# Dilated attention on one Trainium2 core: long and short sequences in turn, the operand splits spread over more steps, and the keys' high halves made by GpSimd

## The chip, the core and the metric

The program runs on one core of a Trainium2 chip. A core has TensorE (PE: matrix products; PEld is its weight load), VectorE (DVE), ScalarE (ACT), GpSimd (POOL) and SyncE (SP, here an issuer of transfers). Each runs its own list of instructions in order; they meet only at semaphores. The metric is the device time in microseconds (us). Before the change three runs took 4597.08, 4600.01 and 4615.36 us: median 4600.01.

## The reference, cut to what matters

One encoder layer over two sequences, of 1024 and 2048 tokens: a projection, a state-space branch, an attention branch, an output projection. The change is in the attention. It computes three windowed attentions of dilation 1, 4 and 16, for 16 heads of 64 channels, and mixes them:

```python
DILATED_PATTERNS = ((128, 1), (512, 4), (2048, 16))
def dilated_window_attention(q, k, v, window, dilation):
    r = window // (2 * dilation)              # 64 keys to either side, in a subsequence
    ...                                       # to_sub: every dilation-th token
    scores = jnp.einsum('nbqhd,nbkhd->nbhqk', qb, kw) * (HEAD_DIM ** -0.5)
    valid = ((jnp.abs(qi[:, :, None] - ki[:, None, :]) <= r)
             & (ki[:, None, :] >= 0) & (ki[:, None, :] < l_sub))
    scores = jnp.where(valid[None, :, None], scores, -jnp.inf)
    lse = jax.nn.logsumexp(scores, axis=-1)
    p = jnp.exp(scores - lse[..., None])
    o = jnp.einsum('nbhqk,nbkhd->nbqhd', p, vw)
```

## The kernel before, in words

The program runs in phases with a barrier between them: projection, convolution, state-space phases, attention, output. Only attention changes.

Attention handles two heads at a time, so there are eight **pairs**. For a pair it works through six **stretches**: one sequence (s = 1 is the 2048-token one, called long here; s = 0 the 1024-token one, short) at one dilation. "Long 4" below is the long sequence at dilation 4. `attention_stretches` sets their order: long 1, long 4, long 16, short 1, short 4, short 16, then the next pair. A long stretch has 8 **steps**, a short one 4; a step handles two tiles of 128 queries for both heads. There are 288 steps. At dilation 1 and 4 a tile of queries meets 256 keys (**banded** steps), at dilation 16 a subsequence has at most 128 tokens, so it meets 128 (**narrow** steps, half the transposes and half the output products).

The score products run in single passes on numbers split in two, high + low. So before a stretch starts, four **pieces** have to be split: query half 0, query half 1, key half 0, key half 1. ScalarE casts the piece to the high part (`split_high`, L1509 to L1518), and GpSimd subtracts it from the original (`split_low`, L1367 to L1373), both reading `nat`, the untouched q and k of the pair, with a stride of the dilation (4 or 16 tokens). A long piece has 1024 elements in each of 128 partitions, a short one 512. Query and key operands have two buffers, used by stretches in turn. `pieces_at` (L1328) says at which step of a stretch the pieces of the next one are made: one in each of the steps 0 to 3 of a long stretch, two in each of the steps 0 and 1 of a short one.

The engines' lists of a step n are:

- TensorE: `turn(n)` transposes the probabilities (L1477), `scores(n + 2)` (L1465), `outputs(n - 1)` (L1493). Before the first scores of a stretch it waits for all four pieces (`a_low`), so that wait stands in step F - 2, where F is the first step of that stretch.
- VectorE: copies the transposed probabilities out of PSUM (L1572), then mask and row minimum of step n + 2 (L1562).
- ScalarE: `copy_o(n - 2)` (L1534), the casts of this step (L1517), then four exponentials of step n + 2 (L1527).
- GpSimd: the subtractions; and at the end of every second stretch one of 16 pieces of the output weights: it issues the load (L1604), waits for it, and splits it with two instructions (L1607, L1610).
- SyncE: loads of `nat` (L1393) and v (L1408, L1413), stores of the outputs (L1425, L1430).

## Time and profile before

| | us |
|---|---|
| median of three runs | 4600.01 |
| the profiled execution | 4615.0 |
| its span, first to last instruction | 4613.4 |
| TensorE busy | 4027.3 |
| VectorE busy | 2015.6 |
| GpSimd busy | 1712.5 |
| ScalarE busy | 1502.0 |

The page of the profile gives busy time of each engine, and the span in 40 slices of 115 us, each digit a share in tenths. Attention is slices 25 to 34 (from zero). The line PEclk is the clock granted to TensorE, in tenths of its full 2.4 GHz: 5 is 1.2 GHz. Matrix products are pipelined and their ends are modelled, so TensorE counts as busy at either clock; how fast it gets on is seen from the count of instructions in a stretch of time. A row of the timeline has start, length, engine, line, operation, the tiles, and in brackets how long the engine was idle before it and who ended that.

### The profile page before, as it was taken

What the parts mean: (1) busy time and instruction counts of PE and PEld (TensorE: products, weight loads), DVE (VectorE), ACT (ScalarE), POOL (GpSimd) and SP (SyncE); (2) the same over time, 40 slices, a digit from 0 to 9 for tenths busy, and PEclk for the clock granted to TensorE, in tenths of its full rate; (3) what the DMA queues carried; (4) which work ended last, traced back from release to release, by engine and by line L of the source; (5) the groups of instructions that cost most, each with busy time, mean ns of one, the idle gap of its engine ahead of it and who ended that gap; (6) DMA issues with size and microseconds to landing.
All of it is one profiled execution on the core that took longest, in us unless ns stands there. A gap on an engine that the chain in (4) does not pass through costs nothing. (4 is left out here: it accounts for less than half of the span.)

```text
span 4613.4 us, 57057 instructions
## 1 busy us (share of the span) xinstructions
PE 4027.3 (87%) x21637; PEld 3219.5 (70%) x21637; DVE 2015.6 (44%) x3716; ACT 1502.0 (33%) x2697; POOL 1712.5 (37%) x965
## 2 busy tenths in 40 slices
PE   6999999999999997325777775999999999799999
PEld 5888878888878886212333332889888898678887
DVE  2000220001300012976888885665565655555554
ACT  3212022121211110320222222776666766422222
POOL 2222432224312232005999997444443333200000
PEclk8999999999999998558888887997897887899999
DMA  5233232323322232557222222343333333434442
GB/s 174 95 98 99 90 125 90 99 94 90 112 91 96 98 108 90 174 168 266 76 92 87 86 93 99 86 116 98 97 112 103 95 101 82 138 142 158 161 157 106
DMA packets 358458, 523.73 MB, mean 114 GB/s; under 512 B 21947, under 2 KB 222723, under 8 KB 354115
## 3 DMA queue, kind: packets, MB, share of 16 engines
q1 hardware_dynamic: 348899, 484.07, 32.7%
q10 hardware_dynamic: 4608, 19.92, 1.4%
q0 software_dynamic: 4736, 16.78, 1.0%
q8 instruction: 145, 2.38, 0.2%
q14 instruction: 70, 0.57, 0.0%
HBM read 336.42 MB, written 184.27 MB: 113 GB/s over the span
## 5 line engine op out<-in xcount | busy, mean ns | idle before, releaser
L313 POOL TENSOR_TENSOR project_w_lo<-project_raw,project_w_hi 128x1024 fp32r<-128x1024 f32 (+1 forms) x204 | 381.1, 1878 | 1001.6 <-ACT project_w_hi L371 1001.6
L443 DVE TENSOR_TENSOR project_part<-project_out,project_table 128x512 f32<-128x512 f32 x48 | 33.2, 691 | 1524.8 <-PE project_out L500 1128.5
L1493 PE MATMUL attn_o_ps<-attn_v,attn_pt_sb 128*128 128x65 f32 x3840 | 557.2, 302 | 0.0
L1527 ACT ACTIVATE attn_p_sb<-attn_p_sb,attn_o_sb 128x256 f32<-128x256 f32 (+1 forms) x1152 | 451.1, 465 | 311.8 <-DVE attn_o_sb L1562 311.8
L1493 PEld LDWEIGHTS attn_o_ps<-attn_v,attn_pt_sb 128*128 128x128 f32 x3840 | 515.3, 214 | 36.2 <-issue 5.7
L1572 DVE COPY attn_pt_sb<-attn_pt_ps 128x1024 f32<-128x1024 f32 (+1 forms) x288 | 301.4, 1047 | 354.6 <-PE attn_pt_ps L1477 354.2
L1562 DVE CUSTOM_DVE_ANT_0 attn_p_sb<-attn_mask,attn_s_ps 128x256 f32<-128x256 bf16 (+1 forms) x1152 | 363.8, 371 | 130.6 <-PE attn_s_ps L1465 112.9
L1371 POOL TENSOR_TENSOR attn_q_lo<-attn_nat,attn_q_hi 128x1024 fp32r<-128x1024 f32 (+1 forms) x96 | 199.0, 2084 | 529.2 <-ACT attn_q_hi L1517 529.2
L500 PE MATMUL project_out<-project_h_hi,project_w_hi 128*128 128x512 f32 x1344 | 339.0, 395 | 29.3 <-DVE project_h_lo L431 29.3
L1024 PE MATMUL ssd_seg<-ssd_spread,masks 128*128 128x512 f32 x384 | 253.7, 803 | 94.5 <-POOL ssd_spread L963 94.4
L500 PE MATMUL project_out<-project_h_hi,project_w_lo 128*128 128x512 f32 x1344 | 334.7, 391 | 0.0
L500 PE MATMUL project_out<-project_h_lo,project_w_hi 128*128 128x512 f32 x1344 | 332.1, 389 | 0.0
L963 POOL TENSOR_TENSOR ssd_spread<-masks,st_a 128x512 f32<-128x512 f32 x192 | 311.3, 1650 | 5.4 <-DMA ssd_skip<-d_skip 4.0
L500 PEld LDWEIGHTS project_out<-project_h_hi,project_w_hi 128*128 128x128 f32 x1344 | 254.1, 190 | 83.1 <-issue 21.1
L371 ACT CAST project_w_hi<-project_raw 128x1024 fp32r<-128x1024 f32 (+1 forms) x204 | 167.7, 845 | 398.4 <-DMA project_raw<-w_in 398.4
L1477 PE MATMUL attn_pt_ps<-ident,attn_p_sb 128*128 128x128 f32 x1920 | 292.4, 297 | 2.1 <-ACT attn_p_sb L1527 2.0
L500 PEld LDWEIGHTS project_out<-project_h_hi,project_w_lo 128*128 128x128 f32 x1344 | 254.6, 189 | 53.8
L500 PEld LDWEIGHTS project_out<-project_h_lo,project_w_hi 128*128 128x128 f32 x1344 | 252.3, 188 | 52.4
L500 PE MATMUL project_out<-project_w_hi,project_h_lo 128*128 128x512 f32 x1152 | 284.5, 389 | 0.0
L500 PE MATMUL project_out<-project_w_hi,project_h_hi 128*128 128x512 f32 x1152 | 284.5, 389 | 0.0
L500 PE MATMUL project_out<-project_w_lo,project_h_hi 128*128 128x512 f32 x1152 | 284.5, 389 | 0.0
L1465 PE MATMUL attn_s_ps<-attn_k_hi,attn_q_hi 64*128 64x256 f32 (+1 forms) x1152 | 204.5, 351 | 74.8 <-POOL attn_k_lo L1371 74.8
(186 smaller groups left out, 6794.0 us busy)
## 6 DMA issues: line engine op xcount, KB each, us to landing
project_raw<-w_in SPq DMA_DIRECT2D x156, 512.0 KB, 4.0
output_parts<-s_o SPq DMA_DIRECT2D x24, 1584.0 KB, 6.5
s_o<-attn_o_sb SPq DMA_DIRECT2D x256, 132.0 KB, 2.0
s_xbcT<-project_stage SPq DMA_DIRECT2D x72, 256.0 KB, 2.0
back_xb<-s_xb ACTq DMA_DIRECT2D x24, 640.0 KB, 6.1
ssd_xb<-s_xb SPq DMA_DIRECT2D x24, 640.0 KB, 4.0
s_v<-project_v_stage SPq DMA_DIRECT2D x48, 260.0 KB, 2.2
s_zs<-project_stage SPq DMA_DIRECT2D x48, 256.0 KB, 2.2
```

What stands on the lines that cost most here:

```text
L313: last = nc.gpsimd.tensor_tensor(low, src, high.bitcast(F32), ALU.subtract)
L371: last = nc.scalar.copy(dst, src)
L500: last = nc.tensor.matmul(dst, lhs, rhs, start=x == 0 and k == 0, stop=x == 2 and k == KT - 1)
L963: last = nc.gpsimd.tensor_tensor(spread[d][b][:, :, :], mask.to_broadcast([P, 4, P]), per_head(chunk_row("a", n)[:, at:at + 4], P), ALU.mult)
L1024: last = nc.tensor.matmul(seg[b][:, :], st["masks"][:, d, :], spread[d][b][:, :, :], start=d == 0, stop=d == 1)
L1371: nc.gpsimd.tensor_tensor(split_cuts(low[st.buf], st, piece, keys), nat_cut(st, piece), split_cuts(high[st.buf], st, piece, keys).bitcast( ...
L1465: last = nc.tensor.matmul(s_ps[n % 2][:, 2 * half + a, 0:st.width], qs[st.buf][rows, queries], ks[st.buf][rows, keys], start=x == 0, stop= ...
L1477: last = nc.tensor.transpose(pt_ps[:, x, cut], p_sb[n % 2][:, x, cut], c["ident"][:, :])
L1493: last = nc.tensor.matmul(o_ps[n % 2][:, x, :], pt_sb[n % 2][:, x, b * P:(b + 1) * P], v[st.buf][:, st.chunk(r, t, b), half * VW:(half + 1 ...
L1527: last = nc.scalar.activation(cut, cut, ACT.Exp, scale=-1.0, bias=o_sb[n % ring][:, x % 2, x // 2, VW:OW])
L1562: nc.vector.tensor_tensor_reduce(out=p_sb[n % 2][:, x, 0:st.width], in0=mask[:, st.strip(t), 0:st.width], in1=s_ps[n % 2][:, x, 0:st.width ...
L1572: nc.vector.tensor_copy(pt_sb[n % 2][:, :, 0:st.width], pt_ps[:, :, 0:st.width]).then_inc(sem["a_pt"], 1)
```

## The change

- The order of stretches is now long 1, short 1, long 4, short 4, long 16, short 16. The split of the next stretch is always made beside one of the other length.
- `splits_at` replaces `pieces_at`. While stretch S (first step F) runs, the next one's pieces are made at steps F - 2, F, F + 2, F + 4 if S is long, and at F - 2, F - 1, F, F + 1 if S is short. The list begins two steps ahead of S itself.
- ScalarE casts only the query pieces. GpSimd makes the high part of a key piece with a `tensor_copy` of its own right ahead of the subtraction; it first waits for both query casts.
- The loads of the output weights are issued by SyncE in step 1 of every long stretch, and GpSimd splits them in step 5; the loop that finished what was left is gone. The loads of `nat` are issued at step 0 of a dilation-16 stretch, for the same sequence of the next pair.

```diff
@@ attention_stretches
-        for s in (1, 0):
-            for pattern in range(len(DILATIONS)):
+        for pattern in range(len(DILATIONS)):
+            for s in (1, 0):
                 stretches.append(Stretch(len(stretches), pair, s, pattern, first))
@@ attention_phase
-        def pieces_at(st, i):
-
-            if st.number + 1 == len(stretches):
-                return ()
-            if st.steps == 4:
-                return ((0, 1), (2, 3), (), ())[i]
-            return (i,) if i < pieces else ()
...
+        splits_at = [[] for _ in steps]
+        for st, following in zip(stretches, stretches[1:]):
+            for piece in range(pieces):
+                splits_at[max(0, st.first - 2 + piece * (2 if st.steps > pieces else 1))].append((following, piece))
@@ gpsimd
             def split_low(st, piece):
                 high, low = ((q_hi, q_lo), (k_hi, k_lo))[piece // 2]
-                pool.wait_ge(sem["a_high"], pieces * st.number + piece + 1)
                 keys = piece // 2 == 1
+                pool.wait_ge(sem["a_key_high" if keys else "a_high"], 2 * st.number + piece % 2 + 1)
...
+            def split_keys_high(st, piece):
+                if piece < 2:
+                    return
+                pool.wait_ge(sem["a_high"], 2 * (st.number + 1))
+                if st.number >= 2 and piece == 2:
+
+                    older = stretches[st.number - 2]
+                    pool.wait_ge(sem["a_scores"], older.first + older.steps)
+                nc.gpsimd.tensor_copy(split_cuts(k_hi[st.buf], st, piece, True), nat_cut(st, piece)
+                                      ).then_inc(sem["a_key_high"], 1)
...
             for n, (st, i) in enumerate(steps):
-                for piece in pieces_at(st, i):
-                    split_low(stretches[st.number + 1], piece)
-                if i == st.steps - 1 and st.number % 2 == 1:
-                    out_weights.load_and_split_next(pool)
-            out_weights.finish_first_half(pool)
+                for following, piece in splits_at[n]:
+                    split_keys_high(following, piece)
+                    split_low(following, piece)
+                if st.steps > pieces and i == st.steps - 3:
+                    out_weights.split_next(pool)
+            pool.wait_ge(sem["first_w_split"], out_weights.pieces)
@@ sync
-                    sp.wait_ge(sem["a_low"], pieces * (st.number - per_round + 3))
+                    sp.wait_ge(sem["a_low"], pieces * (st.number - per_round + 5))
...
-                if i == 1 and st.pattern == 2 and st.number + per_round - 2 < len(stretches):
-                    load_nat(stretches[st.number + per_round - 2])
+                if i == 0 and st.pattern == 2 and st.number + 2 < len(stretches):
+                    load_nat(stretches[st.number + 2])
+                if st.steps > pieces and i == 1:
+                    out_weights.load_next(sp)
@@ scalar
             def split_high(st, piece):
-                dst = (q_hi, k_hi)[piece // 2][st.buf]
+                if piece >= 2:
+                    return
...
-                nc.scalar.copy(split_cuts(dst, st, piece, piece // 2 == 1), nat_cut(st, piece)
+                nc.scalar.copy(split_cuts(q_hi[st.buf], st, piece, False), nat_cut(st, piece)
                                ).then_inc(sem["a_high"], 1)
```

GpSimd's list, before: from the split of pair 1's long 1 (the last of pair 0) to that of its long 4. Rows with 128x1024 belong to a long stretch.

```order
L1371 TENSOR_TENSOR attn_q_lo<-attn_nat,attn_q_hi 128x1024 [waits a_high] x2
L1371 TENSOR_TENSOR attn_k_lo<-attn_nat,attn_k_hi 128x1024 [waits a_high] x2
L1604 DMA out_weights_raw<-w_out 128x512 [waits first_w_split]
L1607 TENSOR_TENSOR out_weights_hi<-out_weights_raw,one 128x512 [waits first_w_in]
L1610 TENSOR_TENSOR out_weights_lo<-out_weights_raw,out_weights_hi 128x512 [waits first_w_hi]
L1371 TENSOR_TENSOR attn_q_lo<-attn_nat,attn_q_hi 128x1024 [waits a_high] x2
L1371 TENSOR_TENSOR attn_k_lo<-attn_nat,attn_k_hi 128x2x512 [waits a_high] x2
```

And after: the split of a long 4 (made beside short 1), that of short 4 (beside long 4), and one piece of the output weights.

```order
L1364 TENSOR_TENSOR attn_q_lo<-attn_nat,attn_q_hi 128x1024 [waits a_high] x2
L1376 CAST attn_k_hi<-attn_nat 128x2x512 [waits a_scores,a_high]
L1364 TENSOR_TENSOR attn_k_lo<-attn_nat,attn_k_hi 128x2x512 [waits a_key_high]
L1376 CAST attn_k_hi<-attn_nat 128x2x512 [waits a_high]
L1364 TENSOR_TENSOR attn_k_lo<-attn_nat,attn_k_hi 128x2x512 [waits a_key_high]
L1364 TENSOR_TENSOR attn_q_lo<-attn_nat,attn_q_hi 128x512 [waits a_high] x2
L1376 CAST attn_k_hi<-attn_nat 128x2x256 [waits a_scores,a_high]
L1364 TENSOR_TENSOR attn_k_lo<-attn_nat,attn_k_hi 128x2x256 [waits a_key_high]
L1376 CAST attn_k_hi<-attn_nat 128x2x256 [waits a_high]
L1364 TENSOR_TENSOR attn_k_lo<-attn_nat,attn_k_hi 128x2x256 [waits a_key_high]
L1624 TENSOR_TENSOR out_weights_hi<-out_weights_raw,one 128x512 [waits first_w_in]
L1627 TENSOR_TENSOR out_weights_lo<-out_weights_raw,out_weights_hi 128x512 [waits first_w_hi]
```

A stretch's split had four GpSimd instructions and has six now: two casts stand between its subtractions. Long and short splits alternate.

ScalarE's list, before, in short 16 of pair 0, where long 1 of pair 1 is made: a COPY opens a step, four ACTIVATE close it.

```order
L1534 COPY attn_o_sb<-attn_o_ps 128x2x2x65 [waits a_o]
L1517 CAST attn_q_hi<-attn_nat 128x1024 [waits a_scores,a_keys_set,a_nat_in1]
L1517 CAST attn_q_hi<-attn_nat 128x1024
L1527 ACTIVATE attn_p_sb<-attn_p_sb,attn_o_sb 128x128 [waits a_max] x4
L1534 COPY attn_o_sb<-attn_o_ps 128x2x2x65 [waits a_o]
L1517 CAST attn_k_hi<-attn_nat 128x1024 x2
L1527 ACTIVATE attn_p_sb<-attn_p_sb,attn_o_sb 128x128 [waits a_max] x4
```

The same split after; these are now the last two steps of long 16.

```order
L1542 COPY attn_o_sb<-attn_o_ps 128x2x2x65 [waits a_o]
L1525 CAST attn_q_hi<-attn_nat 128x1024 [waits a_scores,a_nat_in1]
L1535 ACTIVATE attn_p_sb<-attn_p_sb,attn_o_sb 128x128 [waits a_max] x4
L1542 COPY attn_o_sb<-attn_o_ps 128x2x2x65 [waits a_o]
L1525 CAST attn_q_hi<-attn_nat 128x1024
L1535 ACTIVATE attn_p_sb<-attn_p_sb,attn_o_sb 128x128 [waits a_max] x4
```

The query casts moved two steps ahead and lie one step apart; the key casts are gone from this engine.

## Rows read from the trace of the kernel before

**Rows 1.** The page: busy time by engine, and TensorE's granted clock in 40 slices.
```profile
PE 4027.3 (87%) x21637; PEld 3219.5 (70%) x21637; DVE 2015.6 (44%) x3716; ACT 1502.0 (33%) x2697; POOL 1712.5 (37%) x965
...
PEclk8999999999999998558888887997897887899999
```
**Rows 2.** Windows: busy us (instructions) by engine, granted clock, DMA share, GB/s.
```profile
core 0: us, PE busy (x) PEld busy (x) DVE busy (x) ACT busy (x) POOL busy (x), PEclk, DMA share, GB/s
...
2880.40:3993.80 1113.40, 1072.70 (x9216) 978.16 (x9216) 652.67 (x2592) 755.12 (x1628) 433.62 (x236) 0.86 0.35 97
```
**Rows 3.** Windows: eight banded steps, four narrow ones; three banded, one narrow.
```profile
2917.71:2947.45 29.74, 29.74 (x294) 27.35 (x293) 18.71 (x73) 21.76 (x48) 14.96 (x8) 1.00 0.36 95
...
3108.32:3129.00 20.68, 20.68 (x110) 19.01 (x110) 8.04 (x27) 10.13 (x19) 7.17 (x5) 0.50 0.19 46
2949.03:2958.20 9.17, 9.17 (x98) 8.21 (x98) 5.99 (x35) 6.90 (x22) 2.68 (x3) 1.00 0.77 261
3148.50:3152.73 4.23, 4.23 (x25) 3.78 (x26) 1.61 (x9) 3.50 (x7) 2.96 (x3) 0.50 0.51 108
```
**Rows 4.** TensorE's waits in attention: us in total, times, longest.
```profile
PE attn_s_ps L1465 <- POOL attn_k_lo L1371: 38.2, 18, 4.9
```
**Rows 5.** Timeline: TensorE's wait in pair 1's short 1, twice at short 16.
```profile
3103.27 0.58 PE L1465 MATMUL attn_s_ps<-attn_k_hi,attn_q_hi 64*128 64x256 f32 x2 [2.27 <-POOL attn_k_lo L1371]
...
3008.43 0.58 PE L1465 MATMUL attn_s_ps<-attn_k_hi,attn_q_hi 64*128 64x256 f32 x2 [4.88 <-POOL attn_k_lo L1371]
...
3154.87 0.58 PE L1465 MATMUL attn_s_ps<-attn_k_hi,attn_q_hi 64*128 64x256 f32 x2 [1.08 <-POOL attn_k_lo L1371]
```
**Rows 6.** Windows: stretches of granted half clock in attention, and one of full clock.
```profile
2973.20:2980.10 6.90, 6.90 (x40) 6.34 (x40) 2.07 (x9) 2.08 (x5) 2.36 (x3) 0.51 0.32 82
...
3014.20:3102.90 88.70, 86.64 (x851) 78.84 (x848) 61.77 (x243) 70.45 (x151) 36.88 (x19) 1.00 0.38 108
3102.90:3161.00 58.10, 56.65 (x305) 51.79 (x306) 19.86 (x82) 24.72 (x54) 21.30 (x15) 0.50 0.32 84
...
3249.70:3270.20 20.50, 20.50 (x110) 18.83 (x110) 6.81 (x26) 9.45 (x19) 5.87 (x6) 0.50 0.20 56
...
3287.30:3307.70 20.40, 16.59 (x94) 14.71 (x94) 7.60 (x28) 9.89 (x18) 10.30 (x7) 0.50 0.32 81
...
3393.10:3396.50 3.40, 3.40 (x20) 3.07 (x21) 0.81 (x3) 1.40 (x4) 2.30 (x2) 0.50 0.18 59
```
**Rows 7.** Timeline of pair 0's long 4, first step: TensorE turns, then scores.
```profile
2913.99 1.04 PE L1477 MATMUL attn_pt_ps<-ident,attn_p_sb 128*128 128x128 f32 x8
2914.97 0.39 PE L1465 MATMUL attn_s_ps<-attn_k_hi,attn_q_hi 64*128 64x256 f32 x2
```
**Rows 8.** The same stretch, ScalarE: the casts of two neighbouring steps.
```profile
2914.82 1.97 ACT L1517 CAST attn_q_hi<-attn_nat 128x1024 fp32r<-128x1024 f32 x1
...
2918.56 1.97 ACT L1517 CAST attn_q_hi<-attn_nat 128x1024 fp32r<-128x1024 f32 x1
```
**Rows 9.** The same stretch, GpSimd: the second subtraction.
```profile
2920.61 2.89 POOL L1371 TENSOR_TENSOR attn_q_lo<-attn_nat,attn_q_hi 128x1024 fp32r<-128x1024 f32 x1 [0.86 <-ACT attn_q_hi L1517]
```
**Rows 10.** Timeline before the 4.88 us wait, dilation 1: casts, then subtractions.
```profile
2997.95 1.99 ACT L1517 CAST attn_q_hi<-attn_nat 128x1024 fp32r<-128x1024 f32 x2
```
**Rows 11.** The same place, GpSimd's subtractions of the keys.
```profile
3003.72 4.66 POOL L1371 TENSOR_TENSOR attn_k_lo<-attn_nat,attn_k_hi 128x1024 fp32r<-128x1024 f32 x2
```
**Rows 12.** GpSimd by shape, in attention: busy us, mean ns of one, idle before.
```profile
L1371 POOL TENSOR_TENSOR attn_k_lo<-attn_nat,attn_k_hi 128x1024 fp32r<-128x1024 f32 x48 | 130.2, 2719 | 35.4 <-ACT attn_k_hi L1517 35.4
...
L1607 POOL TENSOR_TENSOR out_weights_hi<-out_weights_raw,one 128x512 fp32r<-128x512 f32 x16 | 16.5, 1031 | 47.9 <-DMA out_weights_raw<-w_out 47.9
...
L1350 POOL MEMSET attn_k_hi<- 128x2560 f32 x2 | 4.5, 2232 | 12.5 <-POOLq L866 12.5
```
**Rows 13.** The loads of nat: time from issue to landing.
```profile
DMA to landing us min/median/max: 4.2/6.2/11.3
```

More of the change, by code:

```diff
@@ L1326, in nat_cut @@
             return rows[:, half * st.dil // 2:(half + 1) * st.dil // 2, :]
-        def pieces_at(st, i):
-            if st.number + 1 == len(stretches):
-                return ()
-            if st.steps == 4:
-                return ((0, 1), (2, 3), (), ())[i]
-            return (i,) if i < pieces else ()
-        def nat_ready(st, pattern=0):
-            return st.number // per_round + 1
+        splits_at = [[] for _ in steps]
+        for st, following in zip(stretches, stretches[1:]):
+            for piece in range(pieces):
+                splits_at[max(0, st.first - 2 + piece * (2 if st.steps > pieces else 1))].append((following, piece))
         def v_ready(st):
@@ L1373, in split_low @@
                                         ).then_inc(sem["a_low"], 1)
+            def split_keys_high(st, piece):
[7 more added lines that the diff above has]
+                                      ).then_inc(sem["a_key_high"], 1)
             for piece in range(pieces):
+                split_keys_high(stretches[0], piece)
                 split_low(stretches[0], piece)
             for n, (st, i) in enumerate(steps):
-                for piece in pieces_at(st, i):
-                    split_low(stretches[st.number + 1], piece)
-                if i == st.steps - 1 and st.number % 2 == 1:
-                    out_weights.load_and_split_next(pool)
-            out_weights.finish_first_half(pool)
+                for following, piece in splits_at[n]:
[4 more added lines that the diff above has]
+            pool.wait_ge(sem["first_w_split"], out_weights.pieces)
         @block.sync
@@ L1434, in _ @@
             load_v(stretches[0])
-            load_nat(stretches[3])
+            load_nat(stretches[1])
             for n, (st, i) in enumerate(steps):
@@ L1508, in split_high @@
             def split_high(st, piece):
-                dst = (q_hi, k_hi)[piece // 2][st.buf]
+                if piece >= 2:
+                    return
                 if piece == 0:
                     act.wait_ge(sem["a_nat_in"][st.s], 32 * (st.number // per_round + 1))
-                    act.wait_ge(sem["a_keys_set"], 2)
                     if st.number >= 2:
@@ L1542, in _ @@
                 copy_o(n - 2)
-                for piece in pieces_at(st, i):
-                    split_high(stretches[st.number + 1], piece)
+                for following, piece in splits_at[n]:
+                    split_high(following, piece)
                 exponentials(n + 2)
@@ L1594, in __init__, with cut, load_next, split_next @@
         self.pieces = D_SSD // P * D // CW
-        self.next = 0
-    def load_and_split_next(self, pool):
-        nc, sem, n = self.nc, self.sem, self.next
+        self.loaded = self.split = 0
+    def cut(self, n):
+        return n // 2, slice(n % 2 * CW, (n % 2 + 1) * CW)
+    def load_next(self, sp):
+        if self.loaded == self.pieces:
+            return
+        k, cols = self.cut(self.loaded)
+        after(sp, self.sem["first_w_split"], self.loaded)
+        sp.dma_start(self.raw[:, :], self.rows[:, k, cols]).then_inc(self.sem["first_w_in"], 16)
+        self.loaded += 1
+    def split_next(self, pool):
+        nc, sem, n = self.nc, self.sem, self.split
         if n == self.pieces:
             return
-        k, cut = n // 2, slice(n % 2 * CW, (n % 2 + 1) * CW)
-        after(pool, sem["first_w_split"], n)
-        pool.dma_start(self.raw[:, :], self.rows[:, k, cut]).then_inc(sem["first_w_in"], 16)
+        k, cols = self.cut(n)
         pool.wait_ge(sem["first_w_in"], 16 * (n + 1))
-        nc.gpsimd.tensor_tensor(self.hi[0][:, k, cut], self.raw[:, :], self.one.to_broadcast([P, CW]), ALU.mult
+        nc.gpsimd.tensor_tensor(self.hi[0][:, k, cols], self.raw[:, :], self.one.to_broadcast([P, CW]), ALU.mult
                                 ).then_inc(sem["first_w_hi"], 1)
         pool.wait_ge(sem["first_w_hi"], n + 1)
-        nc.gpsimd.tensor_tensor(self.lo[0][:, k, cut], self.raw[:, :], self.hi[0][:, k, cut].bitcast(F32), ALU.subtract
+        nc.gpsimd.tensor_tensor(self.lo[0][:, k, cols], self.raw[:, :], self.hi[0][:, k, cols].bitcast(F32), ALU.subtract
                                 ).then_inc(sem["first_w_split"], 1)
-        self.next += 1
-    def finish_first_half(self, pool):
-        while self.next < self.pieces:
-            self.load_and_split_next(pool)
-        pool.wait_ge(self.sem["first_w_split"], self.pieces)
+        self.split += 1
 def output_phase(nc, sem, c, x_parts, y_parts, weights, norm_f, scratch):
@@ L1898 @@
     "f_scaled", "f_rest", "f_cb", "f_zeroed", "f_added", "f_norm_steps", "f_root", "f_m_part", "f_kept",
-    "f_y_steps", "a_keys_set", "a_mask_steps", "a_high", "a_low", "a_scores", "a_max", "a_p", "a_turned", "a_pt",
+    "f_y_steps", "a_keys_set", "a_mask_steps", "a_high", "a_key_high", "a_low", "a_scores", "a_max", "a_p", "a_turned", "a_pt",
     "a_o", "a_o_copied", "first_w_split", "first_w_hi", "first_w_in",
```

## The prediction

> **What bounds the kernel now.** I read the page first: TensorE is busy for 87% of the span, and its granted clock falls in places from slice 25 on, where attention runs [rows 1]. A window over attention, first to last score product, gives 1113.4 us, with a mean clock of 0.86 [rows 2]. So I asked two things: what a step costs at each clock, and what TensorE waits for.
>
> At full clock eight banded steps take 29.74 us, 3.72 each, and four narrow ones 9.17, 2.29 each; TensorE has no gap in either window. At half clock three banded steps take 20.68, 6.89 each, and a narrow one 4.23 [rows 3]. No other engine sets a step. A pair has 24 banded and 12 narrow steps, 24 x 3.72 + 12 x 2.29 = 116.8 us, and eight pairs 934. Attention takes 1113, so 179 us are lost, and they have two names.
>
> The first: TensorE waits 38.2 us in 18 waits, all for GpSimd's last key subtraction [rows 4]. Eight of them are the 2.27 us kind, in step 2 of short 1, where short 4's scores begin. Three are 4.88 us and some 1.08, in short 16, where the next pair's long 1 begins [rows 5]; three are 0.27.
>
> The second: half clock. Each of the eleven waits of 2.24 us or more ends in it, and the clock falls nowhere else in attention. The 2.27 us wait ends at 3103.27, and half clock is granted from 3102.90 to 3161.00; the full-clock stretch ahead of it, 88.7 us long, holds no wait of note [rows 5, 6]. The 1.08 us waits stand inside such stretches. They last 58 us four times (pairs 1, 4, 5, 6), 20.5 twice, 3.4 once and 6.9 four times, 303 us in all. At half clock the engine does 3.72/6.89 = 0.54 of the work, so 0.46 x 303 = 139 us are lost. With 38.2 that is 177, which closes the account. The small waits are cheap; what follows them is not.
>
> The clock comes back in banded steps, sometimes after one and sometimes not after five; in narrow steps at half clock it never did: the 58 us stretches run through the narrow steps of short 16 and end when the banded scores of the next long 1 are back.
>
> **Order of stretches.** Score, transpose and output work is the same, 934 us. The old order gave a long stretch's split the 8 steps of another long one, except once a pair. Now each of the three long splits has to be made beside a short stretch, in 4 steps.
>
> **A long split beside a short banded stretch** (long 4 beside short 1, long 16 beside short 4). The two query casts fall in neighbouring banded steps, as before in long 4's preparation of long 16. There the first of the two steps begins at 2913.99 and TensorE is ready for scores 0.98 later [rows 7]. The casts start at 2914.82 and 2918.56 [rows 8], and the second query subtraction ends at 2920.61 + 2.89 = 2923.50 [rows 9]. Then come, on GpSimd alone and one behind the other, cast c, subtraction 2.9, cast c, subtraction 2.9, and some 0.2 for the two waits between them: done at 2929.5 + 2c. TensorE asks four steps after the first begins: 2913.99 + 4 x 3.72 + 0.98 = 2929.85. The wait is 2c - 0.3, with about 0.1 of semaphore 2c - 0.2.
>
> What is c, a strided fp32 cast of 1024 elements on GpSimd? The trace before has no such operation. From below, the memset: 2232 ns for 2560 elements [rows 12], so 0.95 us for 1024, with no input read. From above the strided two-input subtraction itself, 2.9 [rows 9]; the multiply by a broadcast value, 1031 ns for 512 [rows 12], makes 2.0. The cast reads one stream where the multiply also reads a constant, but it reads with a stride. I take 1.6, between memset and multiply, and 1.1 where the dilation is 1. The wait is then 3.0 us, between 1.7 and 5.6.
>
> The Trainium skill, GPSIMD Engine Reference, section 3.1, puts loops that read one input at 1.03 cycles per element, some 1.0 us for 1024 elements. By that estimate c is 1.0, the wait 1.8, and the sum 19 us less. The same section's 2.6 cycles for two inputs gives 2.3 us, and the dilation-1 subtraction took that: 4.66 for two [rows 11].
>
> **The long split beside short 16.** Before, casts start at 2997.95 [rows 10], and TensorE asks at 3008.43 - 4.88 = 3003.55, 5.6 later. The list now starts two narrow steps sooner, so 5.6 + 4.6 = 10.2 us are there. Needed are the second query subtraction (its cast waits for the next step) by 6.4, then two of 2.33 [rows 11] and two casts of 1.1: 13.5. It would be a wait of 3.3 us at full clock; at half clock four steps last 17 us and there is none.
>
> **Short splits** beside a long stretch have 8 steps for some 10 us of work: hidden, 18.4 us of waits gone at short 1, and short 16's too.
>
> **What a wait drags behind it.** The wait for long 16 stands in step 2 of short 4. By all eleven cases before, a wait of 3.0 us drops the clock. What follows is one and a half banded steps, then the twelve narrow steps of long 16 and short 16 together, where half clock has never ended [rows 3, 6]. The price: 1.5 x 3.17 + 12 x 1.94 = 28 us, with the wait 31 per pair.
>
> The wait for long 4 stands in step 2 of short 1; ten banded steps follow. Seven of the eleven stretches before were short, 10 us in the mean: 3.0 + 0.46 x 10 = 7.6 us. The other four lasted 58: 3.0 + 27 = 30. Two thirds and one third give 15; I take 13, since a long one swallows the wait for long 16. Together 44 a pair, 352 us for eight.
>
> **Small parts.** ScalarE loses 96 key casts, 125 us of its work, but no step waits for it: nothing. At the start, GpSimd's first split grows by two casts ahead of the first scores: + 2 us. The output weights' loads leave GpSimd (16 issues of 0.6 us) and no longer make it wait for them; they stand on SyncE's queue ahead of a store, whose output ring of six gives cover: nothing; without that cover 24 x 0.5 us. The load of `nat` for the next short 1 is issued at the start of short 16 and wanted two steps on, with a landing of 4.2 to 11.3 us [rows 13] against some 6.5 at full clock and 12 at half. At half clock, where I expect narrow steps, it is hidden; else up to 3 us for seven pairs, 21.
>
> **The sum.** Against the profiled execution: 4615 - 177 + 352 + 2 = 4792. That execution lies 15 us over the median of 4600, because the length of the half-clock stretches varies; the sum replaces them all, so I leave the 15 in the uncertainty. Forecast 4790 us, slower by 4%, own range 4745 (all stretches behind long 4's wait short: 8 x 38.6 = 309) to 4840 (half of them long: 398).
>
> **Rivals.** First, the other side: faster. The new waits do not drop the clock, because they come out near 1.7 us, and nothing before lies between 1.08, which stood in half clock already, and 2.24. Then 16 x 3.0 + 8 x 3.3 = 74 us are lost, and fewer if c is small: 4615 - 177 + 74 + 2 = 4514. It decides at the size of wait that still keeps the clock. For it: the waits would be smaller than any that fell. Against: c would have to be at memset's price. The Trainium skill, TensorE: Matmul & The Clock Gate, Part 1, section What's actually happening, says the ramp penalty is under 1% of a typical kernel's span; that would be 46 us here, and by it the result would be near 4560. This trace shows 139 us, 3%, so it does not hold here, and I give this side 12%.
>
> Second, half of them drop it (c near 1.0, waits of 1.8): between the two, (309 + 60) / 2 = 185, so about 4645: 12%.
>
> Third, the strided cast is as dear as the subtraction: waits of 5.6, 16 x 2.6 = 42 more, 4832: 13%.
>
> Fourth, half clock is caught in the banded steps as well, from short 1 to the next long 1, as it was for five steps in four pairs: 12 x 3.17 + 28 + 3 = 69 us a pair, 552: about 4990. Against: in ten steps it has longer to come back. 8%.
>
> **How the numbers follow.** My forecast has 55%. Faster is the first rival, 12%; a measurement of this kernel tells 0.5%, 23 us, and within that lies only part of the second, 3%; slower holds 85%. The range 4640 to 4880 leaves out the first and the fourth, 20%.
>
> **What would show it.** In the profile after: TensorE waits for the key subtraction in step 2 of short 1 and of short 4 in each pair, 2 to 4 us, and no longer for short splits; GpSimd's cast of 128x1024 at 1.0 to 2.0 us; half clock granted over long 16 and short 16 with about 50 us for their twelve steps in most pairs; attention near 1290 us; ScalarE's busy time down by 125 us. I am wrong if the cast is under 0.9 us, if those waits are there and the clock stays, or if narrow steps at half clock win it back.

## The result, and the profile after

Four runs of the changed kernel took 4790.22 to 4820.89 us, median 4807.27; four of the kernel before on the same chip 4595.44 to 4615.36, median 4598.55. The ratio is 1.0448, with a 95% interval of 1.0406 to 1.0490: slower. The forecast was 4790, range 4640 to 4880. A run over 1.5% above the fastest of its kernel counts as slow (four of after_lead3's ten below, two of order_spread's ten, one each of weights_only's and wait_banded's); the ratios, and the spreads told below, leave such runs out, the medians are of all runs.

The profiled execution took 4819.63 us. The page of the kernel after:

```profile
PE 4221.9 (88%) x21637; PEld 3396.1 (70%) x21637; DVE 2014.1 (42%) x3716; ACT 1396.6 (29%) x2601; POOL 1827.2 (38%) x1045
...
PEclk8999999999999995578888866777877786589999
```

Beside [rows 1]: the same 21637 products keep TensorE busy for 195 us more, since more of them ran at a lower clock; ScalarE has 96 instructions fewer and GpSimd 80 more. Attention is slices 24 to 34 here (from zero), and the clock row is at 5 to 8 in every one of them, where the row before has a 9 in three. Windows of the kernel after, columns as in [rows 2]: the whole of attention (it runs to the last output product, as the window of [rows 2] does, 5 to 9 us beyond the last score product), then pieces of pair 1 (the wait before long 4's scores ends at 3111.93, the one before long 16's at 3163.76), then one of pair 0.

```profile
2875.97:4197.44 1321.47, 1266.17 (x9216) 1153.66 (x9216) 657.16 (x2592) 651.79 (x1534) 542.74 (x314) 0.72 0.30 82
3110.00:3120.20 10.20, 8.27 (x48) 7.69 (x48) 2.68 (x9) 2.08 (x5) 3.36 (x2) 0.50 0.22 57
3120.20:3164.60 44.40, 41.03 (x401) 37.57 (x397) 28.53 (x99) 27.16 (x59) 25.24 (x14) 1.00 0.31 83
3164.60:3236.30 71.70, 71.70 (x399) 64.54 (x398) 27.49 (x136) 29.76 (x80) 29.17 (x22) 0.50 0.37 104
3181.40:3215.20 33.80, 33.80 (x193) 30.21 (x193) 12.98 (x72) 15.24 (x42) 13.61 (x10) 0.50 0.29 80
2922.30:3072.50 150.20, 150.14 (x810) 136.97 (x812) 56.87 (x234) 58.36 (x139) 50.16 (x32) 0.50 0.26 72
```

Attention took 1321.5 us where it took 1113.4 [rows 2]: 208 us more, and the whole difference. It began 4.4 us sooner in this execution, and the output phase took 1.0 us more: 4615.4 - 4.4 + 208.1 + 1.0 = 4820.1, against 4819.6 measured. Its mean clock is 0.72 where it was 0.86. In pair 1 half clock lasts 10.2 us after the first wait, 44.4 us of full clock follow, and after the second wait it lasts 71.7 us; eight narrow steps in there take 33.80, 4.23 each, as in [rows 3]. TensorE's waits in attention, and the two of pair 1 (start, us, instruction, [idle before it and what ended it]):

```profile
PE attn_s_ps L1473 <- POOL attn_k_lo L1364: 53.8, 15, 3.8
```

```profile
3111.93 0.58 PE L1473 MATMUL attn_s_ps<-attn_k_hi,attn_q_hi 64*128 64x256 f32 x2 [3.77 <-POOL attn_k_lo L1364]
...
3163.76 0.33 PE L1473 MATMUL attn_s_ps<-attn_k_hi,attn_q_hi 64*128 64x128 f32 x2 [3.37 <-POOL attn_k_lo L1364]
```

Where 18 waits made 38.2 us [rows 4], 15 now make 53.8, and none of them stands before a short stretch: eight before long 4 (3.77 to 3.81 us), seven before long 16 (3.31 to 3.37). Each of the 15 is followed by half clock. GpSimd's timeline ahead of the first of the two shows what TensorE waited for; hardly a gap is left from 3101.90 on:

```profile
3099.06 2.89 POOL L1364 TENSOR_TENSOR attn_q_lo<-attn_nat,attn_q_hi 128x1024 fp32r<-128x1024 f32 x1 [0.90 <-ACT attn_q_hi L1525]
3101.90 2.07 POOL L1376 CAST attn_k_hi<-attn_nat 128x1024 fp32r<-128x1024 f32 x1
3104.05 2.88 POOL L1364 TENSOR_TENSOR attn_k_lo<-attn_nat,attn_k_hi 128x1024 fp32r<-128x1024 f32 x1
3106.87 2.08 POOL L1376 CAST attn_k_hi<-attn_nat 128x1024 fp32r<-128x1024 f32 x1
3109.03 2.85 POOL L1364 TENSOR_TENSOR attn_k_lo<-attn_nat,attn_k_hi 128x1024 fp32r<-128x1024 f32 x1
```

The account. Stretches of half clock in attention were 303 us before and are 729 now: 150.2 once (pair 0), 10.2 five times, 23.9 and 44.4 after long 4's waits; 61 to 96 (the last reaches 32 us beyond attention) after long 16's seven. 0.46 x 426 = 196, and 15.6 us more of waits: 212, against 208 measured.

### The profile page after: what moved, and what is told of

Its sections match the earlier page's. It is cut to its first block and busy times, and to the rows that moved or that the text cites. A ratio compares the mean times of both kernels' runs of the same rounds, so it can differ in the third digit from the quotient of the medians.

```text
span 4818.0 us, 57101 instructions
## 1 busy us (share of the span) xinstructions
PE 4221.9 (88%) x21637; PEld 3396.1 (70%) x21637; DVE 2014.1 (42%) x3716; ACT 1396.6 (29%) x2601; POOL 1827.2 (38%) x1045
## 5 line engine op out<-in xcount | busy, mean ns | idle before, releaser
L1501 PE MATMUL attn_o_ps<-attn_v,attn_pt_sb 128*128 128x65 f32 x3840 | 650.3, 335 | 0.0
L1501 PEld LDWEIGHTS attn_o_ps<-attn_v,attn_pt_sb 128*128 128x128 f32 x3840 | 604.2, 246 | 40.7 <-issue 6.3
L1485 PE MATMUL attn_pt_ps<-ident,attn_p_sb 128*128 128x128 f32 x1920 | 338.0, 327 | 1.1 <-ACT attn_p_sb L1535 1.1
L1473 PE MATMUL attn_s_ps<-attn_k_hi,attn_q_hi 64*128 64x256 f32 (+1 forms) x1152 | 231.6, 397 | 92.6 <-POOL attn_k_lo L1364 92.6
L1485 PEld LDWEIGHTS attn_pt_ps<-ident,attn_p_sb 128*128 128x128 f32 x1920 | 292.0, 184 | 1.6 <-ACT attn_p_sb L1535 1.4
```

What stands on the lines that cost most here:

```text
L1473: last = nc.tensor.matmul(s_ps[n % 2][:, 2 * half + a, 0:st.width], qs[st.buf][rows, queries], ks[st.buf][rows, keys], start=x == 0, stop= ...
L1485: last = nc.tensor.transpose(pt_ps[:, x, cut], p_sb[n % 2][:, x, cut], c["ident"][:, :])
L1501: last = nc.tensor.matmul(o_ps[n % 2][:, x, :], pt_sb[n % 2][:, x, b * P:(b + 1) * P], v[st.buf][:, st.chunk(r, t, b), half * VW:(half + 1 ...
```

## The experiments

All kernels are the changed one with edits; each was compared with the kernel before on its own chip (medians there: 4604.8, 4592.7 and 4604.8 us). "Waits" are TensorE's for the key subtraction within attention, "half" is granted half clock there; both come from the one profiled execution of each kernel, the medians from all runs.

| kernel | order | lead | keys | median us (runs) | ratio, 95% interval | attention | waits | half |
|---|---|---|---|---|---|---|---|---|
| before | old | 0 | ScalarE | 4599 (4) | 1 | 1113 | 38.2 | 311 |
| after | new | 2 | GpSimd | 4807 (4) | 1.0448 (1.0406 to 1.0490) | 1321 | 53.8 | 738 |
| spread_only | old | 2 | ScalarE | 4477 (4) | 0.9709 (0.9671 to 0.9748) | 975 | 11.5 | 47 |
| order_only | new | 0 | ScalarE | 4892 (4) | 1.0637 (1.0587 to 1.0686) | 1388 | 99.7 | 815 |
| keys_only | old | 0 | GpSimd | 4655 (4) | 1.0107 (1.0053 to 1.0161) | 1156 | 54.1 | 375 |
| order_spread | new | 2 | ScalarE | 4604 (10) | 0.9962 (0.9917 to 1.0007) | 1108 | 30.7 | 309 |
| spread_keys | old | 2 | GpSimd | 4467 (4) | 0.9694 (0.9641 to 0.9748) | 968 | 9.1 | 42 |
| weights_only | old | 0 | ScalarE | 4603 (10) | 0.9973 (0.9930 to 1.0015) | 1119 | 40.5 | 316 |
| lead3 | old | 3 | ScalarE | 4451 (6) | 0.9680 (0.9640 to 0.9720) | 953 | 0 | 13 |
| order_lead3 | new | 3 | ScalarE | 4471 (4) | 0.9725 (0.9673 to 0.9777) | 974 | 12.0 | 58 |
| order_lead3_w3 | new | 3 | ScalarE | 4440 (4) | 0.9636 (0.9585 to 0.9687) | 940 | 1.3 | 4 |
| after_lead3 | new | 3 | GpSimd | 4597 (10) | 0.9946 (0.9900 to 0.9992) | 1039 | 29.1 | 162 |
| wait_narrow | old | 3 | ScalarE | 4645 (4) | 1.0104 (1.0049 to 1.0159) | 1152 | 25.8 | 416 |
| wait_banded | old | 3 | ScalarE | 4534 (5) | 0.9863 (0.9797 to 0.9930) | 1062 | 26.9 | 201 |

"Lead" is the step rule: 0 is the old one (pieces begin with the stretch before), 2 the changed one, 3 starts one step sooner still beside short stretches. The model of the prediction, 934 us + waits + 0.46 x half, gives each of the fourteen to within 21 us, eleven of them to within 8 (order_only, 1409 against 1388, is the worst). The half clock of the table counts in 3 to 9 us at attention's very start, which the 303 and 729 above leave out.

Of the twelve expectations below seven gave a range that holds the measured median. order_spread landed between the two ranges given for it, order_lead3 6 us above its range, wait_banded 6 us below, order_lead3_w3 10 us under the one value given; after_lead3 came out 87 us above its range.

### One part of the change at a time

The three switches, as edits of the changed kernel (the new order's own load rules for `nat` go with the first):

```diff
-        for pattern in range(len(DILATIONS)):
-            for s in (1, 0):
+        for s in (1, 0):
+            for pattern in range(len(DILATIONS)):
...
-splits_at[max(0, st.first - 2 + piece * (2 if st.steps > pieces else 1))]
+splits_at[st.first + (piece if st.steps > pieces else piece // 2)]
...
-                    split_keys_high(following, piece)
                     split_low(following, piece)
...
-                if piece >= 2:
-                    return
+                dst = (q_hi, k_hi)[piece // 2][st.buf]
```

**spread_only**: first and third (old order, ScalarE's key casts; the new step rule stays).

> The old order of stretches and the key casts on ScalarE, with the new step rule (a split starts two steps before the running stretch) and the new loading of the output weights. Clock theory (each wait of 2 us or more for GpSimd drops TensorE to half clock, and that is what costs): short 1 now makes short 4 in four banded steps with a lead of 14.9 + 1.0 us against some 13 of work, and short 16 makes long 1 with 10.2 us against 9.4 + 1.1 of work plus the pause between the query casts; the waits fall from 2.27 and 4.88 us to about 0 and 1, no fall of the clock follows, and of the 177 us lost in attention 130 to 160 come back: 4440 to 4480 us. Rival (half clock is the narrow steps' own doing, the waits only mark the place): the 2.27 us waits go but the clock still falls at the end of long 16; only some 30 us come back, 4570.

**order_only**: second and third.

> The new order of stretches alone, with the old step rule (two pieces in each of the first two steps of a short stretch) and the key casts on ScalarE. Clock theory: a long split beside a short one has only two steps of lead, 7.4 + 1.0 us, and takes 2.1 + 4 x 2.9 = 13.7, so TensorE waits 5.5 to 6.5 us for long 4 and for long 16 in every pair, and half clock holds through the narrow steps: slower than the whole change, 4830 to 4900 us. Rival (the key casts on GpSimd are what costs, the order is harmless): within 30 us of before, 4600.

**keys_only**: first and second.

> The old order and the old step rule, with the keys' high parts cast by GpSimd. Clock theory: GpSimd's chain for short 4 grows by two casts of 1.1 us, so the wait in short 1 grows from 2.27 to 4 us, that in short 16 from 4.88 to 6 to 7; the number of falls of the clock stays, a third one may come for short 16: 20 to 70 us slower than before, 4620 to 4670. Rival (GpSimd's casts are the cost of the whole change): most of the 209 us, 4750 or more.

**order_spread**: third alone.

> The whole change with the key casts left on ScalarE. The casts then lie in four neighbouring steps beside GpSimd's subtractions, and the last subtraction of a long split ends about 1.2 us after TensorE asks, instead of 3.4 to 3.8. It asks whether a wait between 1.1 and 2 us drops the clock. If it does: half clock through the narrow steps again, 4720 to 4790. If it does not: waits of 16 x 1.2 and small ones, 4470 to 4500.

TensorE's waits in attention of spread_only, order_only, keys_only and order_spread, in that order:

```profile
PE attn_s_ps L1460 <- POOL attn_k_lo L1364: 11.5, 14, 1.1
```
```profile
PE attn_s_ps L1460 <- POOL attn_k_lo L1364: 99.7, 22, 6.3
```
```profile
PE attn_s_ps L1473 <- POOL attn_k_lo L1364: 54.1, 22, 4.0
```
```profile
PE attn_s_ps L1460 <- POOL attn_k_lo L1364: 30.7, 21, 1.9
```

The step rule alone makes the kernel 128 us faster, within the range that the clock theory gave. GpSimd's key casts alone, in the old order with the old step rule, cost 50 us (4605 to 4655, a ratio of 1.0107), with 22 waits of 1.5 to 4.0 us. The order alone makes it 288 us slower: the long splits beside short stretches, started as late as the old step rule starts them, wait about 6 us (6.05 before long 4, 5.8 before long 16). Order and step rule together undo each other, to no difference. And with them in place GpSimd's casts cost the last 203 us by the medians of two chips (4604 to 4807; the ratios, 0.9962 and 1.0448, part by 4.9%), with 15 waits of 3.3 to 3.8 us where 21 of 1.1 to 1.9 stood.

**spread_keys**: the first switch alone (old order; step rule and GpSimd's casts stay).

> The old order, the new step rule with its lead of two, key casts on GpSimd: the whole change without the new order. Beside short 1, short 4's pieces are 512 long: 0.8 + 1.1 + 2 x 1.5 within two steps, then 2 x (1.1 + 1.5): done before TensorE asks, so the 0.2 to 0.7 us of the kernel with casts on ScalarE go. Before long 1 the chain is two casts of 1.04 longer, but the query casts only, without keys, come sooner: a wait of 1.1 to 3. Clock theory: 4460 to 4510 us, since only banded steps follow. Rival (GpSimd's 125 us of casts cost by themselves): 4600.

```profile
PE attn_s_ps L1473 <- POOL attn_k_lo L1364: 9.1, 12, 1.1
```

4467 against spread_only's 4477 on another chip, with ratios of 0.9694 and 0.9709: in the old order the same 96 casts on GpSimd cost nothing, though its busy time in attention rises from 427 to 545 us. So it is not GpSimd's load that hurts but where its list is short of time: a strided long split beside a short stretch. Where the casts have eight steps they are free. So they are before long 1, which short 16 still makes: TensorE's wait stays at 1.1 us, since the two casts without a stride, 1.04 us each, fill the 1.27 and 0.83 us in which GpSimd waited for ScalarE's key casts in spread_only.

**weights_only**: all three switches undone; only the output weights' loading by SyncE is left, with their split by GpSimd moved to step 5 of a long stretch.

> The kernel before with only the output weights' loads issued by SyncE and their split in step 5 of a long stretch, all the rest as before. The waits in short 1 and short 16 are not touched: the same time as before within the spread of the half-clock stretches, 4580 to 4620 us. If the transfers or GpSimd's issuing had cost anything: faster by 10 us or more beyond that.

No difference, as priced. But two of its waits speak on the clock. One in pair 4, and the window around it:

```profile
3533.95 0.39 PE L1460 MATMUL attn_s_ps<-attn_k_hi,attn_q_hi 64*128 64x256 f32 x2 [2.24 <-POOL attn_k_lo L1364]
```
```profile
3450.00:3560.00 110.00, 107.11 (x1056) 97.75 (x1052) 72.93 (x289) 84.68 (x186) 49.44 (x28) 1.00 0.40 111
```

The size of wait that dropped the clock every time before [rows 5, 6] kept it here, and again 130 us later.

### Take the waits away, then put one back

**lead3**: old order, ScalarE's key casts, and the splits beside a short stretch one step sooner.

```diff
-st.first - 2 + piece * (2 if st.steps > pieces else 1)
+st.first - (2 if st.steps > pieces else 3) + piece * (2 if st.steps > pieces else 1)
```

> The old order, key casts on ScalarE, the new step rule with one change: beside a short stretch the four pieces start three steps ahead of it, not two. The waits of the kernel with a lead of two (0.2 to 0.7 us in short 1, 1.1 us in short 16, of which three of seven dropped the clock) should be gone: a banded step more is 3.7 us, a narrow one 2.3. Clock theory: no wait, no fall, attention at its 934 us and some 12 for its start: 4445 to 4455 us. Rival (with GpSimd out of the way another engine or a transfer becomes the bound): as with a lead of two, 4470 to 4480.

No wait for the key subtraction is left. What is left is TensorE's waits for ScalarE's exponentials, which neither the prediction nor the model counts, and one of them, 0.81 us, is followed by 10.2 us of half clock:

```profile
PE attn_pt_ps L1472 <- ACT attn_p_sb L1522: 7.6, 14, 1.1
```
```profile
3194.22 0.65 PE L1472 MATMUL attn_pt_ps<-ident,attn_p_sb 128*128 128x128 f32 x4 [0.81 <-ACT attn_p_sb L1522]
```

They are most of what attention of lead3 takes beyond the model (953 against 940):

```profile
2881.09:3833.66 952.57, 943.81 (x9216) 860.36 (x9216) 648.95 (x2592) 749.83 (x1628) 427.20 (x220) 0.99 0.41 113
```

**wait_narrow**: lead3, and GpSimd makes the last key subtraction of long 16 twice more in each pair. The repeats write the same numbers.

```diff
+repeats = 2 if piece == 3 and st.s == 1 and st.pattern == 2 and st.number > 0 else 0
-nc.gpsimd.tensor_tensor(...).then_inc(sem["a_low"], 1)
+for n in range(repeats + 1):
+    last = nc.gpsimd.tensor_tensor(...)      # each repeat waits for the one before
+last.then_inc(sem["a_low"], 1)
```

> The kernel with the old order and the lead of three, and in each pair GpSimd repeats the last key subtraction of long 16 twice, 5.8 us more ahead of long 16's scores, of which some 2.6 are covered: one wait of about 3.2 us a pair, right ahead of the eight narrow steps. Nothing else differs. Clock theory: the clock falls and stays down over all eight narrow steps, 1.5 x 3.17 + 8 x 1.94 + 3.2 = 23.5 us a pair, and longer where the banded steps of the short sequence do not bring it back: 190 us and up, 4640 to 4680. Rival (a wait costs its own length): 8 x 3.2 = 26 us, 4475.

**wait_banded**: the same with `st.pattern == 1`: the wait stands before long 4, with banded steps behind it.

> The same repeat for long 4 instead of long 16: the same wait of about 3.2 us, once in pairs 1 to 7 and in pair 0, but with ten banded steps behind it. Clock theory: the clock falls each time, and comes back after 7 to 58 us, at a point that the place of the wait in time decides: 3.2 + 0.46 x 10 = 8 us to 30 us a pair, 60 to 200 in all, and on the low side since narrow steps follow only later: 4540 to 4600, clearly under the kernel with the wait ahead of the narrow steps. Rival (where the wait stands does not matter): the same time as that kernel.

Waits of wait_narrow, and its second stretch of half clock:

```profile
PE attn_s_ps L1467 <- POOL attn_k_lo L1368: 25.8, 8, 3.2
```
```profile
3079.20:3130.40 51.20, 50.50 (x284) 45.80 (x284) 18.18 (x90) 22.68 (x57) 15.89 (x13) 0.50 0.27 85
```

The same of wait_banded, with a short and a long stretch:

```profile
PE attn_s_ps L1467 <- POOL attn_k_lo L1368: 26.9, 8, 3.4
```
```profile
3158.20:3168.40 10.20, 9.10 (x51) 8.32 (x52) 3.10 (x12) 2.08 (x5) 6.13 (x4) 0.50 0.05 13
3284.50:3390.30 105.80, 105.24 (x566) 96.10 (x568) 39.13 (x162) 45.39 (x101) 28.62 (x19) 0.50 0.21 64
```

This is the core of the explanation, shown by itself. Eight waits of 3.2 us ahead of narrow steps cost 4645 - 4451 = 194 us, 24 each: 3.2 for the wait itself and 21 for what follows it, some 51 us of half clock (0.46 x 51 would be 23), which in all eight pairs lasts through the eight narrow steps and ends in the banded steps of short 1. Eight waits of the same size ahead of banded steps cost 83 by the median, and are a gamble: in the profiled execution six are followed by 7 to 10 us of half clock, one by 41, one by 106, and the runs spread over 43 us (4520 to 4564) where wait_narrow's spread over 7. So it is not the added work on GpSimd, the same in both, that sets the price, but what runs behind the wait.

**order_lead3**: new order, lead 3, ScalarE's key casts.

> The new order of stretches with the lead of three steps and the key casts on ScalarE. It asks whether the order costs anything where no wait is left. With a lead of two the waits were 1.1 us before long 4 and long 16; 3.7 us more cover them. Clock theory: as the old order with the same lead, 4450 to 4465 us. Rival (the alternation itself costs: loads of nat late for short 1, v loads for a long stretch beside a short one): 4500 or more, with TensorE waiting for something that is not GpSimd.

It leaves seven waits, 2.34 us in five of the seven short 16. GpSimd's timeline shows why:

```profile
2988.11 2.37 POOL L1364 TENSOR_TENSOR attn_q_lo<-attn_nat,attn_q_hi 128x1024 fp32r<-128x1024 f32 x1 [1.25 <-ACT attn_q_hi L1512]
2990.45 1.03 POOL L1611 TENSOR_TENSOR out_weights_hi<-out_weights_raw,one 128x512 fp32r<-128x512 f32 x1
2991.56 1.28 POOL L1614 TENSOR_TENSOR out_weights_lo<-out_weights_raw,out_weights_hi 128x512 fp32r<-128x512 f32 x1
2992.80 2.37 POOL L1364 TENSOR_TENSOR attn_q_lo<-attn_nat,attn_q_hi 128x1024 fp32r<-128x1024 f32 x1
```

The output weights' split, 2.3 us in step 5 of long 16, stands between two query pieces of the next long 1. (There are 16 such pieces, one in each long stretch, so the last falls in pair 5's long 1; the two short 16 after that wait 0.17 and 0.18 us.) **order_lead3_w3** moves it two steps sooner:

```diff
-if st.steps > pieces and i == st.steps - 3:
+if st.steps > pieces and i == st.steps - 5:
```

> The new order with the lead of three and key casts on ScalarE, and the output weights' split in step 3 of a long stretch instead of step 5, where it stood for 2.3 us between GpSimd's first and second query piece of the next long 1 and made TensorE wait 2.34 us in five of seven pairs. If that was the whole cost of the order: no wait, no fall, 4450 us, as the old order with the same lead. If not: 4470 again.

```profile
2877.20:3816.90 939.70, 936.02 (x9216) 854.45 (x9216) 650.86 (x2592) 749.66 (x1628) 427.12 (x220) 1.00 0.42 115
```
```profile
PE attn_s_ps L1460 <- POOL attn_k_lo L1364: 1.3, 7, 0.3
```

4439.65 us (4438.00 to 4443.46), ratio 0.9636: the fastest kernel of the study, faster than the kernel before and than the changed one, with attention at 939.7 us where the steps alone make 934. The new order shows no cost once next to no wait is left in it. Whether it is better than the old one is not shown: the old order with the weights' split moved too was not run, and lead3's waits for ScalarE (7.6 us) are 1.3 us here.

**after_lead3**: the whole change, GpSimd's casts included, with lead 3 and the weights' split moved.

> The whole change, all three parts kept, with the pieces beside a short stretch started three steps ahead instead of two; the output weights' split moves from step 5 to step 3 of a long stretch, out of the way of the first piece. The waits before long 4 and long 16 were 3.77 and 3.37 us; a banded step more is 3.72, so 0 to 0.1 is left. Before long 1, 10.2 + 2.3 us of lead stand against 13.5 of work: 1.0 us, of which a few drop the clock for some 10 us in banded steps. Clock theory: 4455 + 7 x 1 + 3 x 5 = 4475, 4460 to 4510 us, over 300 us under the change. Rival (GpSimd's key casts or the order cost by themselves): 4600 or more. Rival (nat for short 1 comes late once narrow steps run at full clock): TensorE waits for ScalarE or the queries at short 16, 4500 to 4540.

```profile
PE attn_s_ps L1473 <- POOL attn_k_lo L1364: 29.1, 21, 2.2
```

Here I was wrong: I expected 0 to 0.1 us of wait, by one more banded step of 3.72. Measured were 21 waits: eight before long 4 (1.32 to 1.62 us), eight before long 16 (0.84 to 0.89), five before long 1 (2.22). The first query cast may not start before the scores of the stretch that last used its buffer are done. That is the long stretch two back, and TensorE makes its last scores in that very step; so the lead of a third step is worth 2.5 us, not 3.72 (from the second query cast to TensorE's turn 11.25 us became 13.75). The first query cast of pair 1's long 4 shows it, waiting 1.11 us for those scores:

```profile
3051.60 2.07 ACT L1525 CAST attn_q_hi<-attn_nat 128x1024 fp32r<-128x1024 f32 x1 [1.11 <-PE attn_s_ps L1473]
```

The median fell from 4807 to 4597, a ratio of 0.9946 that hardly parts from no change, and the runs spread over 4543 to 4610: two of the eight 0.87 us waits before long 16 were followed by half clock in the profiled execution, 58 us each. That execution was the fastest of the ten, with a mean granted clock of 0.912 over the whole run, where the run of 4610 us had 0.897. Others thus had more half clock; in which stretches is not shown, since only the one was traced.

## Why the prediction was right, step by step

**The step model** (3.72 and 2.29 us at full clock, 6.89 and 4.23 at half): right; it carries all fourteen executions.

**The waits**: right in place and kind. TensorE waited in step 2 of short 1 and of short 4, and in no short 16 and for no short split. The size was off: 3.0 us forecast, 3.77 to 3.81 and 3.31 to 3.37 measured. The formula was right: with the measured cast of 2.07 before long 4 it gives 2 x 2.07 - 0.2 = 3.9, and with 1.96 before long 16 3.7. What was mis-sized is c, the time of one of GpSimd's strided casts. In attention of the kernel after, by shape (busy us, mean ns of one):

```profile
L1364 POOL TENSOR_TENSOR attn_k_lo<-attn_nat,attn_k_hi 128x1024 fp32r<-128x1024 f32 x46 | 124.6, 2708 | 3.7
L1376 POOL CAST attn_k_hi<-attn_nat 128x1024 fp32r<-128x1024 f32 x46 | 79.2, 1721 | 0.0
L1364 POOL TENSOR_TENSOR attn_k_lo<-attn_nat,attn_k_hi 128x512 fp32r<-128x512 f32 x48 | 69.2, 1441 | 3.8
...
L1376 POOL CAST attn_k_hi<-attn_nat 128x512 fp32r<-128x512 f32 x48 | 44.5, 928 | 0.0
```

The mean of 1721 mixes 1.04 us at dilation 1 (1.1 forecast) with 2.08 at dilation 4 and 1.96 at dilation 16 (1.6 forecast). The answer stood in my own rows and I passed by it: ScalarE's cast of the same piece with a stride took 1.97 [rows 8], without one 1.99 for two [rows 10]. The stride doubles a one-input copy there, and it doubles it on GpSimd too. I bounded by other operations on the same engine, where the same operation on the other engine was nearer.

The Trainium skill, GPSIMD Engine Reference, section 7, says that reads whose step is over 8 bytes cost about half as much again on GpSimd. By that estimate 1.04 would become 1.56; here a step of 16 bytes doubled the copy, and raised the subtraction from 2.34 to 2.88, by a quarter. The direction agrees, the size doesn't, and it depends on the operation.

**What a wait drags behind it, before long 16**: right. Forecast 31 us a pair; measured 23.5 of waits and 0.46 x 459 = 211 of half clock in seven pairs, 34 a pair. The forecast of 1.5 banded and 12 narrow steps at half clock is 61.1 us long; measured were 61.4 twice, 64.9 twice and 71.7 twice, and 95.6 in the last pair.

**Before long 4**: right in the mean by luck in the parts. Forecast 13 us a pair; in seven pairs 26.5 of waits and 0.46 x 119 = 55, so 12. I had a third of them long; two of seven were, in part.

**Pair 0** went by the fourth rival: half clock from long 4's wait through short 16, 150.2 us, 3.8 + 69 = 73 us where the rival had 69 and the forecast 44. It accounts for 29 of the 37 us by which attention's losses (389) exceed the forecast's (352). I gave that rival 8% as all pairs or none; it came in one pair of eight.

**The rivals.** The first (faster, no falls) needed waits near 1.7; order_spread made such waits, 1.1 to 1.9 us, and landed between: some fall, some don't, 4604. The second (half of the waits keep the clock) did not occur: all 15 were followed by half clock. Nor did the third (cast as dear as the subtraction, waits of 5.6). Half clock in attention cost 0.46 x 729 = 335 us here, 7% of the time. The under 1% of the Trainium skill, TensorE: Matmul & The Clock Gate, Part 1, section What's actually happening, is said of the ramp, the half clock that a kernel starts with. I took it for a bound on all half clock, and it is none on what follows a wait in mid-kernel.

**Small parts.** ScalarE lost 105 us rather than 125, and nothing followed from it. GpSimd's first split costs 2.2 us more at attention's start (TensorE's one wait there went from 36.6 to 38.8 us), 2 forecast. `nat` landed in time, weights cost nothing (weights_only: 0.9973, interval 0.9930 to 1.0015).

**Slips in the working**, none of which moved the forecast. The memset's 2232 ns for 2560 elements make 0.89 us for 1024, not 0.95, so the lower bound of the wait is 1.6. The low end of my own range adds up to 4615 - 177 + 309 + 2 = 4749, not 4745. The second rival adds up to 4615 - 177 + 185 + 2 = 4625, not 4645; it lies outside the range, which then leaves out 32% and not 20%. The Trainium skill's 1.03 and 2.6 cycles (GPSIMD Engine Reference, section 3.1) make 0.88 and 2.2 us for 1024 elements at its 1.2 GHz, by estimate, where I wrote 1.0 and 2.3, the times that the trace of the kernel after has for a whole instruction without a stride (1.04 and 2.35).

**One premise fell**, though it did no harm: that each wait of 2.24 us or more ends in half clock. All eleven did in the one execution I had. And TensorE's waits for ScalarE, which I left out, can drop the clock too; see below.

## What to carry to other kernels

Where TensorE is the bound, price a short wait by the steps that run behind it at a lower granted clock, not by its own length: 3.2 us cost 24 here, because the narrow steps behind it never won the clock back: in all fourteen profiled executions every stretch of half clock in attention ended where banded scores were being made, or lasted beyond attention's scores. So the slack of the list that feeds it is read at its shortest place, not from the feeding engine's busy share: the same casts cost nothing beside eight steps and 203 us beside four. And take the price of an operation that the trace lacks from the same operation on the neighbouring engine with the same stride, before other operations on the same engine.

## What the runs showed of the hardware that I had not expected

All waits of TensorE for the key subtraction that began at full clock, in the fourteen profiled executions, and how many had half clock granted from within the wait or soon after it (2.7 us after its end at the latest; no other fall came within 7 us):

| wait, us | waits | followed by half clock |
|---|---|---|
| 0.15 to 0.75 | 28 | 0 |
| 0.75 to 1.2 | 31 | 10 |
| 1.2 to 1.8 | 24 | 12 |
| 1.8 to 2.3 | 22 | 20 |
| over 2.3 | 68 | 68 |

TensorE's waits for ScalarE's exponentials do the same: of the eight of 0.8 us or more that began at full clock, six were followed by half clock (0.81 to 1.62 us; in spread_only, keys_only, spread_keys, lead3 and twice in weights_only). No fall in attention stands without a wait of 0.8 us or more of either kind.

The same wait can go either way in one execution. In order_spread, 1.12 us before long 16 in pair 2, which kept the clock, and the same in pair 3, which lost it for 64.9 us:

```profile
3230.22 0.33 PE L1460 MATMUL attn_s_ps<-attn_k_hi,attn_q_hi 64*128 64x128 f32 x2 [1.12 <-POOL attn_k_lo L1364]
...
3357.98 0.33 PE L1460 MATMUL attn_s_ps<-attn_k_hi,attn_q_hi 64*128 64x128 f32 x2 [1.12 <-POOL attn_k_lo L1364]
```
```profile
3359.60:3424.50 64.90, 64.90 (x364) 58.30 (x363) 24.11 (x122) 31.21 (x79) 18.79 (x11) 0.50 0.39 109
```

That 1.1 us can cost 0 or 30 us is also how I read the spread from run to run: 55 to 68 us where waits of 0.8 to 2.3 us stand (before, order_spread, weights_only, after_lead3), 5 to 12 over four and six runs where no wait for the key subtraction above 0.3 us does (order_lead3_w3, lead3). Where the waits of 1.1 us stand ahead of banded steps, and a fall costs 3 to 8 us, it is 11 and 14 over four runs (spread_only, spread_keys). The mean granted clock of the runs fits: in order_spread the runs of 4551 and 4615 us had 0.913 and 0.901, and 0.012 less clock are 0.024 x 4600 = 110 us more of half clock, 51 of the 64 us by the price of 0.46. What decides it in a given pair, and why half clock among banded steps ends after 10 us in one pair and after 41, 106 or 150 in another, stays open; no run here held all else fixed and moved only the time at which a wait begins.
